# A two-block transformer kernel: hkT written by ScalarE, the first two turned sections earlier, and the six dilated q/k chunks turned by VectorE and DMAs instead of TensorE

## The reference

```python
# second block, one layer's mixer (h is 256 x 1024)
hq, hf, hi, hg, aq, ak, av, ga, gb = split(h @ w_in)   # 21 chunks of 512 columns
f   = lb + (1.0 - lb) * sigmoid(hf)
k_a = 1.0 - f                                          # "hkT" in the kernel
log_f = log(f)                                         # "log_decay"
...
q_b = apply_rope(rms(heads(aq)) * qn, cos, sin)        # 3 groups x 4 heads x 128
k_b = apply_rope(rms(heads(ak)) * kn, cos, sin)
# apply_rope: x * cos + concat([-x2, x1]) * sin, x1 and x2 the halves of a head
# attention of group g on tokens t - j * dilation, dilation 1, 4, 16
```

## Time and profile before

| | us |
|---|---|
| median of 3 runs (2657.18 to 2657.87) | 2657.8 |
| the profiled execution | 2656.8 |
| its span | 2655.0 |
| PE busy | 2645.1 |
| DVE busy | 1967.1 |
| ACT busy | 1427.8 |
| POOL busy | 166.1 |

### The profile page before, as it was taken

The page is one execution under the profiler, slowest core; times in us unless marked ns, Lnnn a source line. Parts: engine busy times, 40 slices in busy tenths (PEclk is TensorE's granted clock), DMA queues, the critical chain, the costliest instruction groups (busy, mean ns, idle before and its releaser), DMA issues.

```text
span 2655.0 us, 42138 instructions
## 1 busy us (share of the span) xinstructions
PE 2645.1 (100%) x15660; PEld 2240.7 (84%) x15660; DVE 1967.1 (74%) x2660; ACT 1427.8 (54%) x2021; POOL 166.1 (6%) x98
## 2 busy tenths in 40 slices
PE   9999999999999999999999999999999999999999
PEld 8888888888888888888888888888888888888888
DVE  6777767777777876777776888567777769876676
ACT  5446565445446565544545767554454466765543
POOL 0000000000000000000000132000000012210000
PEclk9999999999999999999999999999999999999999
DMA  7556455655555545556555754546555665454553
GB/s 239 190 175 207 150 169 169 202 190 195 193 193 196 166 160 183 176 190 196 180 190 190 230 167 165 185 149 205 190 178 192 212 199 185 162 188 159 186 190 130
DMA packets 324380, 489.26 MB, mean 184 GB/s; under 512 B 17312, under 2 KB 204064, under 8 KB 324256
## 3 DMA queue, kind: packets, MB, share of 16 engines
q1 hardware_dynamic: 323968, 487.47, 56.0%
q10 hardware_dynamic: 288, 0.07, 0.0%
HBM read 478.02 MB, written 1.05 MB: 180 GB/s over the span
## 4 chain that ended last, share of the span: by engine, by line
PE 94%; DVE 2%; ACT 2%; issue 1%; DMA 0%; POOL 0%; SPq 0%; ACTq 0%; DVEq 0%
PE bank L371 48%; PE bank L573 22%; PE bank L571 12%; PE bank L476 5%; PE bank L941 2%; PE bank L984 1%; PE bank L390 1%; DVE w_low L333 1%; ACT w_high L328 0%; PE bank L976 0%; DVE log_decay L2040 0%; PE bank L1647 0%; POOL decay L2118 0%; PE bank L1167 0%; ACT log_decay L1802 0%
## 5 line engine op out<-in xcount | busy, mean ns | idle before, releaser
L333 DVE TENSOR_TENSOR w_low<-raw,w_high 128x2048 fp32r<-128x2048 f32 x435 | 1008.3, 2319 | 397.5 <-ACT w_high L328 397.1
L328 ACT ACTIVATE w_high<-raw 128x2048 fp32r<-128x2048 f32 x435 | 831.1, 1912 | 474.5 <-PE bank L571 243.0
L371 PE MATMUL bank<-w_high,xT_parts 128*128 128x512 f32 x2304 | 739.4, 395 | 0.0
L573 PE MATMUL bank<-xT_parts,w_high 128*128 128x512 f32 x2560 | 618.6, 391 | 0.0
L573 PEld LDWEIGHTS bank<-xT_parts,w_high 128*128 128x128 f32 x2560 | 472.1, 188 | 92.2
L371 PEld LDWEIGHTS bank<-w_high,xT_parts 128*128 128x128 f32 x2304 | 432.6, 188 | 89.9
L371 PE MATMUL bank<-w_low,xT_parts 128*128 128x512 f32 x1152 | 448.7, 389 | 0.0
L571 PEld LDWEIGHTS bank<-xT_parts,w_low 128*128 128x128 f32 x2560 | 334.5, 191 | 16.7
L571 PE MATMUL bank<-xT_parts,w_low 128*128 128x256 f32 x2560 | 339.4, 282 | 0.0
L668 ACT ACTIVATE siluT<-gateT 128x256 f32<-128x256 f32 x160 | 66.8, 417 | 407.3 <-DVE gateT L724 406.9
L371 PEld LDWEIGHTS bank<-w_low,xT_parts 128*128 128x128 f32 x1152 | 216.6, 188 | 42.6
(11 more groups left out here) (308 smaller groups left out, 2684.7 us busy)
## 6 DMA issues: line engine op xcount, KB each, us to landing
raw<-in_w_in SPq DMA_DIRECT2D x288, 512.0 KB, 4.6
raw<-in_ffn_w_in SPq DMA_DIRECT2D x176, 512.0 KB, 4.5
raw<-in_ffn_wd SPq DMA_DIRECT2D x88, 512.0 KB, 4.1
raw<-in_ffn_w_out SPq DMA_DIRECT2D x88, 512.0 KB, 4.1
raw<-in_ffn_wg SPq DMA_DIRECT2D x86, 512.0 KB, 3.8
raw<-in_ffn_wu SPq DMA_DIRECT2D x86, 512.0 KB, 4.7
raw<-in_w_out SPq DMA_DIRECT2D x32, 512.0 KB, 4.2
raw<-in_w_branch_a SPq DMA_DIRECT2D x16, 512.0 KB, 5.3
```

What stands on the lines that cost most here:

```text
L328: nc.scalar.activation(wh[slot][:], raw[slot][:], ACT.Copy).then_inc(high_done[slot], 1)
L333: nc.vector.tensor_tensor(wl[slot][:], raw[slot][:], wh[slot][:].bitcast(F32), ALU.subtract).then_inc(low_done[slot], 1)
L371: mm = pe.matmul(o[:, 0:n], x[:, rows], w[slot][:, col + j * n:col + (j + 1) * n], start=start and first, stop=stop and last)
L573: mm = pe.matmul(bank[:], wh[s][:, w], xhl[:, kt, :, :], start=kt == 0, stop=False, skip_group_check=True)
```

## The change

1. `hkT` is written by ACT right behind `log_decay` (steps 6 and 12) instead of by DVE (steps 6 and 11); DVE now waits for it at levels 0 and 8.
2. First mixer: ACT makes the chunk copy of steps 2 and 4 ahead of the high half, DVE rotates and turns ahead of the low half, SP sends the squares one unit earlier (7 and 9). One of ACT's fills (`sq_head`) also moves ahead of the high half.
3. The gains go into tables of cosine and sine per chunk, `rope_tables`, that POOL writes with two instructions of 128x256 behind its power. On DVE the chunk is then rotated in three instructions instead of four, and the multiplication by the gain at odd steps goes for queries and becomes one instruction instead of eight for keys.
4. The rotation stands behind the low half of its step, and a transposition of the 32x32 squares follows it on DVE. SP sends the squares home with four DMAs per chunk ahead of the load of unit 30+2a. ACT copies the chunk at step 27+2a (the last at step 36) from that tile: four instructions of 128x256 that pick one residue each, or one of 128x1024 for chunk 3. PE's eight transposes per chunk are gone.
5. The two products `hg_gate` (L2060) are made at steps 29 and 31 instead of both at 29.

```diff
@@ mix1_sp / mix1_act / mix1_dve
-                if u in (8, 10):
-                    si = u // 2 - 4
+                if u in (7, 9):
+                    si = (u - 7) // 2
...
-                if 0 < u < MIX1 - 1:
+                if 0 < u < MIX1 - 1 and u not in (2, 4):
                     split_high(act, 1, slot_of(u + 2), lay, mix_use(u + 2))
...
+                if u in (2, 4):
+                    split_high(act, 1, slot_of(u + 2), lay, mix_use(u + 2))
...
+                if u in (2, 4):
+                    si = u // 2 - 1
+                    rotated(dve, lay, si)
+                    dve.wait_ge(rope_done, at(lay, 4, si + 1))
+                    squares_turned(stage[si], ssq[si]).then_inc(ssq_turned, 1)
                 if 0 < u < MIX1 - 1:
                     split_low(dve, 1, slot_of(u + 2), lay, mix_use(u + 2))
@@ mix2_sp
+                a, odd = divmod(u - AQ0 - 8, 2)
+                if odd == 0 and 0 <= a < 6:
+                    sp.wait_ge(asq_turned, at2(lay, 6, a + 1))
+                    if a > 1:
+                        sp.wait_ge(sec_out2, at2(lay, 6, a - 1))
+                    squares_home(sp, asq, aland[a], aT_in[a % 2])
@@ mix2_tail (PE)
-            a, odd = divmod(u - AQ0 - 3, 2)
-            if odd == 0 and 0 <= a < 6:
-                pe.wait_ge(rope_done2, at2(lay, 6, a + 1))
...
-                for i in range(2):
-                    tr = turn_tokens(pe, wk[2 + i], stg[a % 2], 2 * i)
-                tr.then_inc(sec_T2, 1)
@@ mix2_act
                         a.then_inc(lnf_done, 1)
+                        for h in range(4):
+                            hd = 4 * hf + h
+                            a = nc.scalar.activation(kT[:, hd, :].rearrange("p (t k j) -> p t k j", t=TT, k=4),
+                                                     hland[1][:, :, h].rearrange("p k t j -> p t k j"), ACT.Identity,
+                                                     bias=omlb[:, hd:hd + 1], scale=lbn[:, hd:hd + 1])
+                        a.then_inc(k_done, 1)
...
+                a, odd = divmod(u - AQ0 - 5, 2)
+                if u == ATT0:
+                    a, odd = 5, 0
+                elif a > 4:
+                    odd = 1
+                if odd == 0 and a >= 0:
+                    act.wait_ge(aT_in[a % 2], at2(lay, 192, 64 * (a // 2 + 1)))
+                    dst = (aqT, akT)[a // 3][:, 4 * (a % 3):4 * (a % 3) + 4, :]
+                    if a == ATT_GROUPS:
+                        r = nc.scalar.activation(dst.rearrange("p h (t k j) -> p (h t) k j", t=TT, k=4), aland[a][:].rearrange("p k h t j -> p (h t) k j"), ACT.Copy)
+                    else:
+                        for c in range(4):
+                            r = nc.scalar.activation(dst.rearrange("p h (t c k i) -> p (h t) c k i", t=TT, c=4, k=4)[:, :, c],
+                                                     aland[a][:].rearrange("p k h t (i c) -> p (h t) k i c", c=4)[:, :, :, :, c], ACT.Copy)
                     r.then_inc(sec_out2, 1)
@@ mix2_dve
+                    x, xr, xs = [y[:].rearrange("p t (h s e) -> p t h s e", h=ATT_HEADS, s=2) for y in (stg[a % 2], rtm, rsq)]
...
+                    dve.wait_ge(tab_done, at2(lay, 6, a + 1))
+                    nc.vector.tensor_tensor(xr, x[:, :, :, ::-1, :], sin, ALU.mult)
+                    if a > 0:
+                        dve.wait_ge(aT_in[(a - 1) % 2], at2(lay, 192, 64 * ((a + 1) // 2)))
+                    link(dve, nc.vector.tensor_tensor(xs, x, cos, ALU.mult))
+                    link(dve, nc.vector.tensor_tensor(stg[a % 2][:], rsq[:], rtm[:], ALU.add))
+                    squares_turned(stg[a % 2], asq).then_inc(asq_turned, 1)
...
-                        dve.wait_ge(hT_in[1], at2(lay, 128, 64 * (hf + 1)))
-                        for h in range(4):
-                            hd = 4 * hf + h
-                            a = nc.vector.tensor_scalar(kT[:, hd, :].rearrange("p (t k j) -> p t k j", t=TT, k=4),
...
-                        for i in range(8):
-                            r = nc.vector.scalar_tensor_tensor(x8[:, i], x8[:, i], rsa[:, a, i:i + 1], gain, ALU.mult, ALU.mult)
+                    dve.wait_ge(apow_done, at2(lay, 6, a + 1))
+                    r = nc.vector.tensor_tensor(x8, x8, rsa[:, a, :].unsqueeze(2).broadcast_to((P, 8, DH)), ALU.mult)
@@ mix2_pool
                     nc.gpsimd.tensor_tensor(rsa[:, a, :], msa[:], neghalf[:, 0:8], ALU.pow).then_inc(apow_done, 1)
...
+                    nc.gpsimd.tensor_tensor(tab[:, 0], cos, gain.unsqueeze(1).broadcast_to(each), ALU.mult)
+                    nc.gpsimd.tensor_tensor(tab[:, 1], sin, gain[:, ::-1, :].unsqueeze(1).broadcast_to(each), ALU.mult).then_inc(tab_done, 1)
```

More of the change, by code:

```diff
@@ L130, in mix_use @@
     return FSTEPS + slot_uses(u, slot_of(u))
-LINKS = {1: 58, 2: 30}
+LINKS = {1: 58, 2: 33}
 def build(nc, t):
@@ L252, in build @@
         akT = over("akT", [P, 12, SEQ], 0)
+        asq = over("a_squares", [P, 1024], 74)
+        tabs = [over(f"rope_tables{a}", [P, 2, TT, DH], kib) for a, kib in enumerate((72, 28, 72, 28, 30, 28))]
+        aland = [over(f"a_turned{a}", [P, 4, 4, TT, 32], kib) for a, kib in enumerate((12, 16, 12, 16, 20, 12))]
         ob = over("o_b", [P, TT, 512], 12)
@@ L1826, in mix2_act @@
                     r.then_inc(asq_done, 1)
-                a, odd = divmod(u - AQ0 - 4, 2)
-                if odd == 0 and 0 <= a < 6:
-                    act.wait_ge(sec_T2, at2(lay, NSEC, a + 1))
-                    for i in range(2):
-                        dst = (aqT, akT)[a // 3][:, 4 * (a % 3) + 2 * i:4 * (a % 3) + 2 * i + 2, :]
-                        if a == ATT_GROUPS:
-                            r = nc.scalar.activation(dst, wk[2 + i][:].rearrange("p (k n) -> p k n", k=2), ACT.Copy)
-                        else:
-                            r = nc.scalar.activation(dst.rearrange("p h (t c i) -> p (h t) c i", t=TT, c=4), by_residue(wk[2 + i]), ACT.Copy)
+                a, odd = divmod(u - AQ0 - 5, 2)
[12 more added lines that the diff above has]
+                                                     aland[a][:].rearrange("p k h t (i c) -> p (h t) k i c", c=4)[:, :, :, :, c], ACT.Copy)
                     r.then_inc(sec_out2, 1)
                 if u in (33, 35):
+                    act.wait_ge(sec_out2, at2(lay, 6, (u - 25) // 2))
                     for kt in range(2 * (u - 33), 2 * (u - 33) + 4):
@@ L1909, in mix2_dve @@
                         dve.wait_ge(hq_out, at2(lay, 2, hf + 1))
+                        dve.wait_ge(k_done, at2(lay, 2, hf + 1))
                         if hf == 0:
@@ L2127, in mix2_pool @@
                     nc.gpsimd.tensor_tensor(rsa[:, a, :], msa[:], neghalf[:, 0:8], ALU.pow).then_inc(apow_done, 1)
+                    if a == 0:
+                        pool.wait_ge(kblk_in, at(lay, 16, 16))
+                    elif a == 1:
+                        pool.wait_ge(A_done, at2(lay, NHG, NHG))
+                    else:
+                        pool.wait_ge(asq_turned, at2(lay, 6, a - 1))
+                    cos, sin = [kblk[:, k:k + TT * DH].rearrange("p (t s e) -> p t s e", t=TT, s=2) for k in (K2_COS, K2_SIN)]
+                    gain = cols[:, C2_QK + a * DH:C2_QK + (a + 1) * DH].rearrange("p (s e) -> p s e", s=2)
+                    each = (P, TT, 2, DH // 2)
+                    tab = tabs[a][:].rearrange("p n t (s e) -> p n t s e", s=2)
+                    nc.gpsimd.tensor_tensor(tab[:, 0], cos, gain.unsqueeze(1).broadcast_to(each), ALU.mult)
+                    nc.gpsimd.tensor_tensor(tab[:, 1], sin, gain[:, ::-1, :].unsqueeze(1).broadcast_to(each), ALU.mult).then_inc(tab_done, 1)
         t_mix = {1: dict(sp=mix1_sp, pe=mix1_pe, act=mix1_act, dve=mix1_dve, pool=mix1_pool),
```

56 lines of the change are left out of this document (13 added, 43 removed).

## The result

| | before | the change |
|---|---|---|
| median, us | 2657.49 (2656.92 to 2657.87, 6 runs) | 2666.74 (2665.49 to 2669.70, 6 runs) |
| the profiled execution | 2656.8 | 2666.8 |
| its span | 2655.0 | 2665.0 |

The forecast was 2661, range 2648 to 2668. The runs of the change also spread four times as far as those of the kernel before, which turned out to matter. All medians are over fast runs: one run of c1 (9796 us) and one of c3 (3255 us), far outside the rest, are left out.

A forecast was written before the change was run, and what follows sets the result against it. PE's own instruction stream was taken as the bound. From the profiled 2656.8 us: -10.4 transposes, -0.7 first mixer, +3.9 keys, +2 x 5.3 wait at unit 36 gave 2660.2; the median being 1.0 higher, about 2661, range 2648 to 2668.

The forecast's parts named there:

- rival D: Last chunk's squares land late and POOL's tables hold DVE longer: 2669 with both, 2665 with either alone; chance 0.23.
- Transposes: Second block's mixer: twelve groups of eight PE transposes removed, 0.87 us each, 10.4 us off PE.
- Chunk 5's chain: Second block's mixer, without the keys' delay: chunk 5 turned at 1667.0, landed at 1671.5, copied by ACT at 1673.5.
- The road: SP's four DMAs bringing chunk 5's squares home: 4.5 us from turned to landed, as in the recurrence.
- The copies: ACT's four copies of chunk 5 after landing: 1.97 us, as the logarithms took.
- The wait at PE: Tail of unit 36, second block's mixer: PE waits 5.3 us per layer for ACT's copies of the last chunk.
- The tables: POOL's table instructions hold DVE 0.5 to 0.6 us each; six count for chunks 3 to 5: +3.3 per layer.
- the forecast's sum: DVE from unit 31's low half to the end of chunk 5's work: 34.15 us plus 1.8, so 35.9, without tables.
- "0.8 to 0.9 us": Sign expected in the profile after: the length of one of POOL's table instructions of 128x256.
- The keys: Recurrence, level 4: `hkT` on ACT delays the exponentials and PE by 1.95 us per layer, +3.9 in all.
- The first mixer: Turning sections earlier removes PE's 0.7 us wait in one layer; later low halves counted as nothing: -0.7.

The follow-up runs named there:

- c1: The change with the whole first mixer put back (SP's, ScalarE's and VectorE's order): 2665.84 us, +7.9 against the kernel before.
- c3: The change with the four `hkT` instructions back on VectorE: 2663.74 us, +6.4 against the kernel before.
- c7: The kernel before, but chunks 0 to 2 turned by VectorE and DMAs with tables, 3 to 5 still by TensorE: 2652.20 us, -5.7.
- the two pairs: Runs differing in one part alone. Keys: the change and c3, c1 and c6. First mixer: the change and c1, c3 and c6. Differences 2.9, 4.1; 1.3, 2.5 us.
- c2: The change with only SP's order of the first mixer put back: 2666.51 us, +9.1 against the kernel before.
- c6: The dilated chunks alone: the change with the first mixer and the keys put back: 2661.77 us, +3.9 against the kernel before.
- c9: The change with a fill of 15 unread matmuls on PE ahead of the wait at the tail of unit 36: 2662.48 us, +5.1 against the kernel before.
- c10: The dilated chunks alone, as in c6, with 15 unread matmuls ahead of the wait at the tail of unit 36: 2657.68 us, -0.2 against the kernel before.
- c5: The change with chunk 5 rotated and turned ahead of the low half of unit 36: 2670.94 us, +13.6 against the kernel before.

## Why the prediction was right or wrong

**The time lay in the range, but not for the reason that put it there.** 2666.7 lies between the two values of rival D (2665 and 2669), the last chunk landing late with dearer tables. That did not happen: the landing took the time that the forecast gave it, and the wait at unit 36 was shorter than the forecast's. What the forecast said of the dilated chunks held within 1 us, and two terms that it had at nothing or less, the clock and the first mixer, made up the difference. That the range reached far enough for them was luck.

- **Transposes, -10.4.** Right: in c7 half of them were worth 5.2 by the sum, and 5.7 were measured.
- **Chunk 5's chain.** The recurrence ran 5.05 us late (1543.86 against 1538.81). With that, the prediction's times are: turned at 1672.05, landed 1676.55, PE goes on at 1678.55. Measured: 1671.4, 1675.9, 1678.31. The road took 4.5 us, as in the recurrence. The copies took 2.32 instead of 1.97.
- **The wait at PE, 5.3 per layer.** Measured 3.9 there and 1.0 at unit 34, together 4.9. The second place was not foreseen. It is the same lateness of VectorE, met two units earlier at `oaT_low`, and does not add to it.
- **The tables, 0.55 per instruction, 3.3 per layer.** Mis-sized: the multiplication takes 1.65 instead of 1.22, the low half 2.61 instead of 2.29, 0.43, 0.75 and 0.75 us for chunks 3 to 5, and `hg_gate` beside chunk 3's 0.44, together 2.4. The stretch from the low half of unit 31 (1633.03) to the end of chunk 5's transposition (1671.38) is 38.35 us, without them 36.0; the forecast's sum was 35.9. "0.8 to 0.9 us" for one of them was a guess between two states: 0.6 alone, 1.6 and more beside VectorE.
- **The keys, +3.9.** Right: PE's wait at unit 13 is 2.10, that at unit 15 still 1.53, and `hkT` holds ScalarE for 1.97 from start to start, where 1.97 was foreseen. The time was 2.9 and 4.1 in the two pairs.
- **The first mixer, -0.7.** Wrong, +1.3 and +2.5 in the medians of the two pairs, +3.0 in the profiled execution. The 0.7 was won. The step that failed is "the load of unit 9 behind eight small DMAs; the halves are done two steps ahead of use, so I count nothing". The eight issues take 5 us of SP, the load left 6.3 us later (857.16 against 850.90), took 8.0 to land, and two steps of cover did not hold that. The half itself was in time for PE. But ScalarE and VectorE work in order, and what stood behind the two halves in their programs, the exponentials and `w_diff`, had no such cover.
- **What no term had: the clock, +4.1.** The sum priced a pause of PE at its own length. Each of the two at unit 36, 3.9 to 4.0 us long, costs its length and then 1.6 to 2.8 us more in the profiled executions of the change, c1, c2, c3 and c6, since TensorE works at 1.2 GHz behind it. c9 and c10 show it by removing nothing but the idling. It also spreads the runs of the change: with the fill 4.2 us become 2.4.

In sum, against the 9.3 measured: -10.4, +9.9 in the two waits near unit 36, +4.1 clock, +3.5 keys, +1.9 first mixer (the middles of the two pairs): +9.0. The last two are the 5.4 us between the change and c6, divided. What the sum really tests is c6: -10.4 + 9.9 + 4.1 = +3.6, and +3.9 was measured.

What the 3.9 us pause would be worth with the squares of chunk 5 also one place earlier on SP was not tried, nor was another place for the keys on ScalarE.

## What to carry to other kernels

Where one engine is busy all the time, price every pause that a change puts into it twice: by its length, and by the slow clock behind it; if the pause can't be removed, a few unread matmuls ahead of the wait keep the clock (4 us here for two pauses of 4). Follow a moved step through every queue that it passes, SP's above all: eight issues of 0.63 us each ahead of a load are 5 us, and the engine that waits for that load holds up everything behind it in its program, not only the work that needs the load. And when work is handed from a full engine to a nearly full one, hand over only as many pieces as the stage has room for: three chunks of six gave all of their gain, the fourth nothing, the last two together cost more than they gave (-5.5 with four, +3.9 with six, -0.2 with six and the clock kept).

## What was not expected of the hardware

- With a pause of 3.9 to 4.0 us the granted clock went to 0.50 in all ten cases (two layers of five profiled executions), and stayed there for 3.4 to 6.8; it fell from 1.8 us before TensorE went on to 0.9 behind. With pauses of 2.0 to 2.7 in the recurrence it fell in the first layer in five of six profiled executions, in the second layer in none, and once behind one of 1.9 in the first mixer (c5). With pauses of 1.6 and less in the recurrence it never fell.
- An addition of 128x1024 on VectorE whose result is written with a stride of 16 bytes took 2.02 us, with consecutive elements 1.23.
- A GpSimd multiplication of 128x256 took 0.64 us alone and mostly 1.6 to 2.7 beside VectorE's, and lengthened those by 0.32 to 0.44 each.
